# Ten gate projections computed in the token mixer instead of six, four of them in pieces, on three PSUM banks for the recurrence

## The reference, cut to what matters

```python
h = x @ w_in                                 # inputs of four branches, 512 channels each
a = pool_mixer(...)                          # trailing means
b = hgrn2_mixer(...)                         # gated linear recurrence
c = gmlp_mixer(...)                          # spatial gating in chunks of 128
d = fox_mixer(...)                           # causal attention with forgetting
br = stack([a, b, c, d])
gates = sigmoid(x @ w_gate + b_gate)         # (512, 4, 1024), from x alone
merged = sum over m of (br[m] @ w_branch[m]) * gates[:, m]
return merged @ w_out
```

## Time and profile before

| | us |
|---|---|
| three runs | 4186.91, 4193.54, 4191.10; median 4191.1 |
| the profiled execution, whole | 4191.99 |
| its span, first to last instruction | 4190.3 |
| PE busy | 3896.6 (93% of the span) |
| DVE, ACT, POOL busy | 2799.5, 1483.8, 1312.4 |
| mean granted TensorE clock | 0.96 of full speed |

### The profile page before, as it was taken

One profiled execution on the slowest core, in us unless ns is written; L12 is line 12 of the kernel. 1 busy time (PEld: TensorE's weight loads), 2 busy tenths in 40 slices (PEclk: granted clock), 3 DMA queues, 4 the chain that ended last, 5 costly groups with the idle time before them and its releaser, 6 DMA issues. The chain is left out here.

```text
span 4190.3 us, 55217 instructions
## 1 busy us (share of the span) xinstructions
PE 3896.6 (93%) x19618; PEld 3407.1 (81%) x19618; DVE 2799.5 (67%) x5400; ACT 1483.8 (35%) x2136; POOL 1312.4 (31%) x1140
## 2 busy tenths in 40 slices
PE   8987899999789999999899878999997899999996
PEld 7865687899788999988778566878997889999885
DVE  3254434479997888877642644343899888888776
ACT  2232322234573333333321323222445633333332
POOL 1010000056574555532100100000666755555321
PEclk9997899999899999999999978999999999999998
DMA  3210323244369999999622103222444699999994
GB/s 141 80 57 1 111 93 113 106 149 174 124 217 360 354 354 338 345 338 333 234 102 80 58 1 118 96 103 106 160 168 147 231 358 355 358 340 344 334 331 173
DMA packets 263243, 836.41 MB, mean 200 GB/s; under 512 B 19617, under 2 KB 68769, under 8 KB 237985
## 3 DMA queue, kind: packets, MB, share of 16 engines
q1 hardware_dynamic: 189344, 565.82, 37.8%
q0 software_dynamic: 73728, 268.47, 17.4%
HBM read 749.81 MB, written 84.41 MB: 199 GB/s over the span
## 5 line engine op out<-in xcount | busy, mean ns | idle before, releaser
L1044 POOL TENSOR_TENSOR ahead_u_low<-merged,ahead_u_high 128x1024 fp32r<-128x1024 f32 x96 | 255.5, 2678 | 1241.4 <-ACT ahead_u_high L1039 1241.4
L87 PE MATMUL bank<-v_high,w_high 128*128 128x512 f32 x1536 | 598.1, 389 | 0.0
L86 PE MATMUL bank<-v_low,w_high 128*128 128x512 f32 x1536 | 598.1, 389 | 0.0
L88 PE MATMUL bank<-v_high,w_low 128*128 128x512 f32 x1536 | 597.4, 389 | 0.0
L1089 POOL DMA_INDIRECT far_rows<-peer_v_dram,far_index x256 | 370.4, 1447 | 503.5 <-DVE x_far L1113 458.9
L1089 POOL DMA_INDIRECT far_rows<-peer_u_rows_dram,far_index x256 | 368.0, 1437 | 346.0 <-DVE far_dots L1095 295.4
L1731 DVE TENSOR_TENSOR v_low<-v_raw,v_high 128x1024 fp32r<-128x1024 f32 x256 | 301.9, 1221 | 231.4 <-ACT v_high L1670 231.4
L1670 ACT ACTIVATE v_high<-v_raw 128x1024 fp32r<-128x1024 f32 x256 | 257.1, 1052 | 499.0 <-PE bank L88 493.4
L86 PE MATMUL bank<-xT_low,u_high 128*128 128x384 f32 x1088 | 372.1, 342 | 19.2 <-ACT hid L1658 10.0
L88 PE MATMUL bank<-xT_high,u_low 128*128 128x384 f32 x1088 | 371.2, 341 | 0.0
L87 PE MATMUL bank<-xT_high,u_high 128*128 128x384 f32 x1088 | 371.1, 341 | 0.0
(11 more groups left out here) (356 smaller groups left out, 8520.4 us busy)
## 6 DMA issues: line engine op xcount, KB each, us to landing
merged<-peer_u_dram SPq DMA_DIRECT2D x128, 1024.0 KB, 7.2
v_raw<-peer_v_dram SPq DMA_DIRECT2D x128, 1024.0 KB, 7.9
gates_scratch<-stage SPq DMA_DIRECT2D x12, 4096.0 KB, 14.4
G<-gates_scratch SPq DMA_DIRECT2D x64, 768.0 KB, 7.8
in_raw<-w_in_dram SPq DMA_DIRECT2D x40, 1024.0 KB, 6.2
mg_raw<-w_merge_dram SPq DMA_DIRECT2D x52, 768.0 KB, 4.2
hidden_scratch<-ahead_hid SPq DMA_DIRECT2D x60, 384.0 KB, 2.4
hid<-hidden_scratch SPq DMA_DIRECT2D x30, 768.0 KB, 7.1
```

Of the source, the lines that this page charges most:

```text
L86: nc.tensor.matmul(out, lh, rl, start=first, stop=False)
L87: nc.tensor.matmul(out, lh, rh, start=False, stop=False)
L88: return nc.tensor.matmul(out, ll, rh, start=False, stop=last)
L1044: eng.tensor_tensor(self.ul[:, c], self.ur[:, c], as_f32(self.uh[:, c]), ALU.subtract).then_inc(self.u_low, 1)
```

## The change

It does five things. The mixer computes ten gate projections; the first six as before. Numbers 6 to 9 (the last two of branch 0 and the first two of branch 1) are multiplied in pieces of 3 to 5 of their 8 steps (3 matmuls a step), placed inside the first attention step of a part, after that step's logits. They all accumulate in bank 3, so a gate begins only when ACT has kept the one before. Their raw weights go through one buffer, `x_far`, which the mixer does not use otherwise; so a load waits for the low half of the gate before. The recurrence's levels, key transposes and state updates use banks 0 to 2 in turn. In the merge, units 6 to 9 take their logits from DRAM; units 8 and 9 are written out.

```diff
+GATES_EARLY = 6
+GATES_AHEAD = 10
...
 merge_stage:
+            ahead = min(max(GATES_AHEAD - KT * m, 0), KT)
+            for n in range(ahead):
+                body(KT * m + n, n, n % 2)
+            if ahead == KT:
                 return
-            with eng.Fori(0, KT // 2) as i:
+            with eng.Fori(ahead // 2, KT // 2) as i:
...
-                        if m == 0 and n < GATES_AHEAD:
+                        if isinstance(n, int) and n < GATES_AHEAD:
                             sp.wait_ge(prods, n + 1)
                             sp.dma_start(gate[:, b, :], a["gate_logits"][n]).then_inc(logits_in[b], 16)
...
 mixer_stage:
+        def raw_gate(n):
+            return gl_raw[:, n % 2] if n < GATES_EARLY else spare[:].rearrange("p (k n) -> p k n", n=P)
         def load_gate(sp, n):
-            if n >= 2:
+            if n > GATES_EARLY:
+                sp.wait_ge(gl_low, n)
+            elif 2 <= n < GATES_EARLY:
                 sp.wait_ge(gl_low, n - 1)
...
+        def bank_of_gate(n):
+            return bank[n % 2] if n < GATES_EARLY else bank[3]
+
+        def multiply_gate(pe, n, start=0, stop=KT):
+            if start == 0:
+                pe.wait_ge(gl_low, n + 1)
+                if n >= GATES_EARLY:
+                    pe.wait_ge(gl_ready, n)
+                elif n >= 2:
+                    pe.wait_ge(gl_ready, n - 1)
+            for k_in in range(start, stop):
...
+            if stop == KT:
+                mm.then_inc(gl_mm, 1)
...
-                def fox(s):
+                def fox(s, between=()):
                     if s + 1 < UNITS:
                         logits(s + 1)
+                    for n, start, stop in between:
+                        multiply_gate(pe, n, start, stop)
                     if 0 <= s - 1 < UNITS:
                         turn(s - 1)
...
+                gates_at = {("level", 0): [(6, 0, 5)], ("level", 1): [(6, 5, 8)], ("level", 2): [(7, 0, 3)],
+                            ("level", 3): [(7, 3, 8), (8, 0, 5)], ("level", 4): [(8, 5, 8), (9, 0, 3)],
+                            ("norm", 0): [(9, 3, 6)], ("end", 0): [(9, 6, 8)]}
...
                     for t in range(NT):
-                        if i:
-                            pe.wait_ge(att_done, NT * (i - 1) + t + 1)
+                        at = NT * i + t
+                        if at >= 3:
+                            pe.wait_ge(att_done, at - 2)
                         elif t == 0:
-                            pe.wait_ge(gl_ready, GATES_AHEAD)
+                            pe.wait_ge(gl_ready, GATES_EARLY)
...
                 for t in range(NT):
-                    pe.wait_ge(att_done, NT * NL + t + 1)
+                    at = NT * (NL + 1) + t
+                    if t < 3:
+                        pe.wait_ge(att_done, at - 2)
+                    else:
+                        pe.wait_ge(kd_kept, t - 2)
...
                     if t < NT - 1:
-                        if t >= 2:
-                            pe.wait_ge(s_upd, t - 1)
+                        if t:
+                            pe.wait_ge(s_upd, t)
...
-                fox_steps(fox, ("norm", 0))
+                fox_and_gates(("norm", 0))
+                for n, start, stop in gates_at[("end", 0)]:
+                    multiply_gate(pe, n, start, stop)
                 pe.wait_ge(o_normed, 1)
...
 ACT:
                     if i == 1:
-                        for n in range(3, GATES_AHEAD):
+                        for n in range(3, GATES_EARLY):
                             keep_gate(act, n)
                     if i:
                         fox_steps(fox, ("level", i - 1))
+                    if i == 2:
+                        keep_gate(act, 6)
...
                 A(flat(tmp[0]), flat(tmp[0]), ACT.Exp).then_inc(lvl_e, 1)
+                keep_gate(act, 7)
                 fox_steps(fox, ("level", NL - 1))
...
                 A(flat(cumb), flat(cumb), ACT.Exp).then_inc(kd_e, 1)
+                keep_gate(act, 8)
                 fox_steps(fox, ("level", NL))
...
                 act.wait_ge(params_in["normg"], 16)
+                keep_gate(act, 9)
```

More of the change, by code:

```diff
@@ L761, in build_program @@
                             peer.release()
-                        mixer_stage(nc, a, layer, sb, mixing, bank, (xh, xl), projT, projN, ffT, ident, lvl_mask, neg_mask, head_sel,
+                        mixer_stage(nc, a, layer, sb, mixing, bank, (xh, xl), x_far, projT, projN, ffT, ident, lvl_mask, neg_mask, head_sel,
                                     pool_rc, scan_keep, one_minus_lb)
@@ L840, in units @@
         def units(eng, m, body):
-            if m == 0:
-                for n in range(KT):
-                    body(n, n, n % 2)
+            ahead = min(max(GATES_AHEAD - KT * m, 0), KT)
+            for n in range(ahead):
+                body(KT * m + n, n, n % 2)
+            if ahead == KT:
                 return
-            with eng.Fori(0, KT // 2) as i:
+            with eng.Fori(ahead // 2, KT // 2) as i:
                 for b in range(2):
@@ L887, in multiply @@
                         pe.wait_ge(w_low, n + 3)
-                        if m or n >= GATES_AHEAD:
+                        if not isinstance(n, int) or n >= GATES_AHEAD:
                             pe.wait_ge(gated, n + 1)
@@ L923, in sigmoids @@
                     def sigmoids(n, dt, b, last=False):
-                        here = m == 0 and n < GATES_AHEAD
+                        here = isinstance(n, int) and n < GATES_AHEAD
                         if here:
@@ L929, in sigmoids @@
                             act.wait_ge(prods, n + 1)
-                        nc.scalar.activation(gate[:, b, :], gate[:, b, :] if here else bank[b][:], ACT.Sigmoid, bias=b_gate[:, dt, m:m + 1] if m == 0 else b_gate[:, ds(dt, 1), m]).then_inc(gated, 1)
+                        nc.scalar.activation(gate[:, b, :], gate[:, b, :] if here else bank[b][:], ACT.Sigmoid, bias=b_gate[:, dt, m:m + 1] if isinstance(dt, int) else b_gate[:, ds(dt, 1), m]).then_inc(gated, 1)
                         if not last:
@@ L1774, in _, with mixer_stage @@
                 split_v(NG - 1, 1)
-def mixer_stage(nc, a, layer, sb, sem, bank, x, projT, projN, ffT, ident, lvl_mask, neg_mask, head_sel,
+def mixer_stage(nc, a, layer, sb, sem, bank, x, spare, projT, projN, ffT, ident, lvl_mask, neg_mask, head_sel,
                 pool_rc, scan_keep, one_minus_lb):
@@ L1868, in high_gate @@
                 act.wait_ge(gl_mm, n - 1)
-            nc.scalar.activation(gl_wh[:, n % 2], gl_raw[:, n % 2], ACT.Copy).then_inc(gl_high, 1)
+            nc.scalar.activation(gl_wh[:, n % 2], raw_gate(n), ACT.Copy).then_inc(gl_high, 1)
         def low_gate(pool, n):
             pool.wait_ge(gl_high, n + 1)
-            nc.gpsimd.tensor_tensor(gl_wl[:, n % 2], gl_raw[:, n % 2], as_f32(gl_wh[:, n % 2]), ALU.subtract).then_inc(gl_low, 1)
-        def multiply_gate(pe, n):
-            pe.wait_ge(gl_low, n + 1)
-            if n >= 2:
-                pe.wait_ge(gl_ready, n - 1)
-            for k_in in range(KT):
-                mm = matmul_split(nc, bank[n % 2][:], (gl_wh[:, n % 2, k_in, :], gl_wl[:, n % 2, k_in, :]),
+            nc.gpsimd.tensor_tensor(gl_wl[:, n % 2], raw_gate(n), as_f32(gl_wh[:, n % 2]), ALU.subtract).then_inc(gl_low, 1)
+        def bank_of_gate(n):
[8 more added lines that the diff above has]
+            for k_in in range(start, stop):
+                mm = matmul_split(nc, bank_of_gate(n)[:], (gl_wh[:, n % 2, k_in, :], gl_wl[:, n % 2, k_in, :]),
                                   (x[0][:, k_in, :], x[1][:, k_in, :]), k_in == 0, k_in == KT - 1)
-            mm.then_inc(gl_mm, 1)
+            if stop == KT:
+                mm.then_inc(gl_mm, 1)
         def keep_gate(act, n):
@@ L1887, in keep_gate @@
                 act.wait_ge(gl_out[n % 2], 16 * (n // 2))
-            nc.scalar.activation(gl_kept[:, n % 2, :], bank[n % 2][:], ACT.Copy).then_inc(gl_ready, 1)
+            nc.scalar.activation(gl_kept[:, n % 2, :], bank_of_gate(n)[:], ACT.Copy).then_inc(gl_ready, 1)
             if n + 2 < GATES_AHEAD:
@@ L1992, in _, with fox_and_gates @@
                         multiply_gate(pe, PE_GMLP)
-                for n in range(PE_GMLP + 1, GATES_AHEAD):
+                for n in range(PE_GMLP + 1, GATES_EARLY):
                     multiply_gate(pe, n)
+                gates_at = {("level", 0): [(6, 0, 5)], ("level", 1): [(6, 5, 8)], ("level", 2): [(7, 0, 3)],
+                            ("level", 3): [(7, 3, 8), (8, 0, 5)], ("level", 4): [(8, 5, 8), (9, 0, 3)],
+                            ("norm", 0): [(9, 3, 6)], ("end", 0): [(9, 6, 8)]}
+                def fox_and_gates(part):
+                    for at, s in enumerate(first_step[part]):
+                        fox(s, gates_at[part] if at == 0 else ())
                 pe.wait_ge(fq_ready, 1)
@@ L2024, in _ @@
                     if t < NT - 1:
-                        if t >= 2:
-                            pe.wait_ge(s_upd, t - 1)
```

(9 more changed lines are left out.)

17 lines of the change are left out of this document (8 added, 9 removed).

## The result

| | before, us | after, us |
|---|---|---|
| four runs, median (lowest to highest) | 4192.32 (4186.91 to 4194.08) | 4126.68 (4124.39 to 4128.96) |
| the profiled execution; its span | 4191.99; 4190.3 | 4124.39; 4122.7 |
| PE busy | 3896.6 (93%) | 3860.1 (94%) |
| mean granted TensorE clock | 0.960 | 0.972 |

The change takes the kernel to 0.9847 of its time, with an interval from 0.9831 to 0.9862: 65.6 us less. The prediction was 4131.0.

A forecast was written before the change was run, and what follows sets the result against it. TensorE bounds the merge, a chain of DVE and ACT work the recurrence. Merge -22.4 + 2.0 and recurrence -13.9 + 0.4 + 3.7 give -30.2 us a layer, twice -60.4: 4131 us, range 4104 to 4164.

The forecast's parts named there:

- the first gap: TensorE's 4.11 us idle gap in the recurrence, ended by ACT; its end was to move by 1.3 us.
- The clock, 13.9: Recurrence: closing TensorE's idle gaps keeps its clock up, saving 13.9 us a layer, of at most 19.4.
- nine groups: Stretches of recurrence matmuls after gaps, each with a predicted saving by the clock, together 19.4 us a layer.
- the fourth gap: TensorE's 8.67 us idle gap in the recurrence, ended by DVE; not filled nearly to the end, DVE later there.
- the fifth gap: TensorE's 8.15 us idle gap in the recurrence, ended by DVE; gate 9 has to wait for ACT there.
- POOL, 3.7: Recurrence: POOL's low halves block DVE, costing 3.7 us a layer: gate 7 1.3, gate 8 0.2, gate 9 2.2.
- The pieces, 0.4: Recurrence: gate pieces overrun their gaps by 0.4 us a layer at full clock, 11.3 at half clock.
- The merge's start, +2.0: Merge: 6 us of waiting at units 8 and 10 instead of 3.7, +2.0 a layer, bounds 0 and +6.
- B: Recurrence clock stays as it is and pieces overrun: -11.3 us a layer, 4168 us; chance 0.19.
- C: Half clock takes the whole recurrence stretch, making the kernel slower: +18.6 us a layer, 4228 us; chance 0.04.
- A: Recurrence clock never falls and POOL is not in the way: -39.4 us a layer, 4112 us; chance 0.14.
- D: Merge gives nothing back because loads hold TensorE; bounded at +6 us, then 4139 us, inside the forecast's range.

The follow-up runs named there:

- low_on_dve_wout: Changed kernel with low halves of gates 6 to 9 on DVE instead of POOL, and output weights loaded before m = 2 instead of m = 1; 4112.66 us.
- keep_earlier: Changed kernel with ACT keeping gate 8 between its two exponentials instead of after them; 4131.24 us.
- fillers_all: Kernel before, with three banks for the recurrence and the same 96 matmuls a layer added in the gaps, results dropped, merge unchanged; 4162.61 us.
- pool_later: Changed kernel with POOL's low halves of gates 7 and 9 waiting for DVE's factors of levels 1 and 4; 4125.86 us.
- rest_filled: Changed kernel with 12 more matmuls a layer, results discarded, in front of gate 9 while TensorE waits for ACT to keep gate 8; 4131.75 us.

## Why the prediction was right

**The sum.** Predicted -60.4 us, measured -65.6 in the medians and -67.6 between the two spans. By its own parts, a layer:

| | predicted | measured, layers 0 and 1 |
|---|---|---|
| merge | -20.4 | -18.4, -20.0 |
| recurrence | -9.8 | -12.9, -13.1 |
| elsewhere | 0 | -3.2 in all |

**What the profile after should show.** The stretch 136 to about 126 us with a clock near 0.9: 123 and 0.93. Gate matmuls 0.233 us apart: yes. A DVE difference of about 2.5 us beside POOL at the first gap: it was 1.61. A rest of 3 to 4 us before gate 9: 3.56, by ACT's keep of gate 8, as worked out. A wait of about 5 us at unit 8 and 1 us at unit 10: 5.12 and 0.42, in layer 1 5.75 and 1.57, with `w_out` issued just ahead as written.

**The mis-sized terms.** *The clock, 13.9.* The measured -12.9 less the pieces' 0.4 and POOL's 2.6 (0.4 for gate 7, 2.2 for gate 9) leaves about 15.9 a layer, and with POOL gone the recurrence fell by 17.6 and 17.8 us in `low_on_dve_wout`, close to the 19.4 that the prediction gave as the upper end. The starts of the prediction's nine groups in layer 0, before less after, add up to the same 15.9. The first five, taken whole as 8.4, gave 7.1: level 1 shrank by 0.9 us and not by 2.2, for the clock fell behind the first rest in spite of its piece. Of the last four, 11.0 and taken half as 5.5, came 8.8: nothing of the 1.8 behind the fourth gap, where TensorE rested 2.87 us and the clock fell; 1.3 of 1.8 in level 4; 5.8 for the 5.4 of the 12 us behind the fifth gap; 1.7 of 2.0 at the end. So the step that was too low is the half taken of the chain behind the fifth gap: the clock there was full and not half, with gate 9's piece between the rest and the chain. `keep_earlier` shows the other order, where the clock there was low (0.57) in layer 0, though not in layer 1. *POOL, 3.7.* Gate 9's 2.2 was right to the tenth (4.48 less 2.29). Gate 7's was 0.4 and not 1.3, for POOL began at 315.87 instead of 316.4 us: half a microsecond earlier leaves less behind the start of DVE's operation. Gate 8's 0.2 was not seen. *The pieces, 0.4.* No piece is a wait of its own; the third gap is closed wholly. *The merge's start, +2.0.* The waits grew by 3.8 us in layer 0 (7.5 against 3.68) and by 2.3 in layer 1 (7.3 against 5.1). The foreseen ones, at units 8 and 10, take 5.5 and 7.3 us for the 6 worked out. Layer 0 has 1.95 us more at 453.79, which was not foreseen; the kernel before had such an early wait too, of 1.55 us, in layer 1 alone. What makes it come and go was not followed. *The range of this case.* Its stated bounds (10 for the clock, 8 for POOL, 6 for the merge's start) add up to 4155 us at the slow end, and not to the 4146 given; the forecast and the range of 4104 to 4164 do not hang on it.

**The rivals.** B (the clock as it is, 4168) fell with the clock of 0.93 and again with `fillers_all`; C (4228) fell with it, for the recurrence became shorter and not longer. A (4112) was wrong for the change, for the clock does fall, in level 1 (0.79 from 324 to 332 us), behind the fourth gap (0.59 from 372 to 378) and at 388 us, and POOL is in the way; but the kernel with POOL out of the way and `w_out` later lands on 4112.7. D's bound held: the waits of the merge's start grew by 3.8 and 2.3 us, under its 6. The Trainium skill's rule ("TensorE: Matmul & The Clock Gate", section "HAM oscillation — how this bites in real kernels"), that the engine must be kept fed between bursts, is borne out by `fillers_all`, whose useless matmuls save 28.4 us. That by "SBUF — State Buffer", section "Who interferes with whom", on VectorE's operations with two SBUF inputs, fits the 4.48 us. The same section says that such a single-input operation is not held unless it is in one of the two-port modes, which it grants to `tensor_scalar` among others; by that rule the `TENSOR_SCALAR` of 2.46 us in `pool_later` was in such a mode. The trace does not name a mode, but the rate fits: the same operation on 128, 256, 384 and 512 elements takes 0.28, 0.35, 0.42 and 0.49 us, 0.5 ns an element, where `TENSOR_TENSOR` needs 1.0 ns (1.22 us for 1024, 2.29 for 2048).

**What stays open.** The 3 us gained outside the two stages, and whether `keep_earlier` and `rest_filled`, 5 us above the change in the median, are slower at all: the intervals overlap, and in their profiles the clock at 340 us was low in both layers, where the change's profile has it full in both. The runs of one kernel lie up to 11 us apart here (4123.31 to 4134.45), about the scatter of a recurrence in both layers. Why the clock falls at 340 us in one execution and not in the next, behind equal rests, no run here shows.

## What to carry to other kernels

Work taken from a stage that TensorE fills and put, in pieces that fit, into the gaps of a stage that waits for other engines pays twice: once for the matmuls taken out, and once for the clock that the gaps no longer bring down; here the second part was some 14 us of 33 a layer, measured by adding the pieces without taking anything out. Look next at what feeds the pieces: an operation on POOL can hold up DVE's work in SBUF beside it, here `TENSOR_TENSOR` and `TENSOR_SCALAR` operations, so a small one is better put on DVE, in a wait it has anyway. Since the granted clock of the same code differs between executions, judge an edit worth a few microseconds by several profiles and both layers. And a large prefetch that filled time beside heavy units must move when those units become light, for it then stands ahead of small loads in the same queue.

## What the runs showed of the hardware

- Beside a POOL `TENSOR_TENSOR` with both inputs in SBUF, DVE's `TENSOR_SCALAR` with one SBUF input stood still too: 2.46 us instead of 0.35 and 1.58 instead of 0.28 (`pool_later`). I had expected it of operations with two SBUF inputs alone.
- After 1.0 us of rest or less, within the attention's logits (two of their four products have only 4 rows of weights), the granted clock fell all the same at about 326 us (level 1 took 4.97 us after the change, against 3.74 at full clock); in `fillers_all`, after 0.60 us of rest at the same place, it stayed at 1.00 from 324 to 332 us. In one execution it was low again at 340 us and in another with the same instructions and rests it was not (0.65 and 1.00).
- 192 matmuls whose results nobody uses made the kernel 28.4 us faster, with a granted clock of 0.92 and 0.93 instead of 0.75 in the 124 and 123 us of the two recurrence stretches.
